# Key and value compression with three products of summed chunks for two neighbouring rows

## The chip, the cores and the metric

One core of one Trainium2 chip runs the whole kernel in one launch. The metric is the device time in microseconds (us), from the median of several runs. Lower is better.

## What is computed

The kernel is one inference step of a decoder with two layers, for a prompt of 512 tokens and for a group of 8 samples with 4 new tokens each, whose past of 2048 tokens lies in pages of 128 tokens. Layer 1 is sparse attention. One of its branches looks at compressed keys and values of the past, and these are computed anew in every step, for each of the 8 samples, from the cached pages:

```python
def compress(x, pos_emb, w1, w2):
    B, L, G, hd = x.shape
    n_chunk = L // CMP_STRIDE
    ch = x[:, :n_chunk * CMP_STRIDE].reshape(B, n_chunk, CMP_STRIDE, G, hd)
    ch = ch.transpose(0, 1, 3, 2, 4).reshape(B, n_chunk, G, CMP_STRIDE * hd)
    half = CMP_STRIDE * hd
    hidden = (ch[:, :-1] @ w1[:half] + ch[:, 1:] @ w1[half:]) + pos_emb.reshape(-1) @ w1
    return jax.nn.gelu(hidden) @ w2
```

Here L is 2048, the stride is 16 tokens, G is 4 heads of 64, so there are 128 chunks with 4 heads each, 1024 numbers long. Row n of the hidden values (256 wide) is chunk n times the first half of w1 plus chunk n+1 times the second half. There are 127 rows for each head. Keys and values each have their own w1 and w2.

## The kernel before

`nsa_compress` (L2043) does this between the prompt's attention and `nsa_decode` (L2225). It works through 16 units: the keys of the 8 samples, then the values of the 8. The order on each engine is written out by hand, and semaphores join them; each engine runs its own list in order.

The reading order `loads` has 18 entries: the key weights, 8 key units, the value weights, 8 value units. Each entry fills one of two slots of the tile `RAWc` (2 MB). A unit's 16 pages come half from SP's queue and half from POOL's (`pages`, L2080); `slot_free` makes a queue wait until the slot's last user has been split. After its own loads, SP also fetches the pages of the selected-block keys of samples 0 and 1 into the tile `KS` (`key_pages`, L2037), which `nsa_decode` reads first.

Each product of 32-bit numbers is made from three products of a high part (a cast to the fp32r type) and a low part (value less high part): high by high, low by high, high by low. ScalarE casts the high part (L2173), VectorE subtracts the low part (L2219). A unit is cut in 8 steps k, each with 128 contraction rows and 512 columns (16 pages x 8 chunks x 4 heads), in tiles `CHi` and `CLo` that hold all 8 steps. The list `jobs` says in which order steps are cut; the value weights' 8 steps alternate with those of the first value unit.

TensorE takes, for each step k, two column halves m of the hidden values and two halves h of w1, three matmuls of 512 or 508 columns (L2150 to L2152), 96 in a unit. They add up in one PSUM bank for each m, and the shift by one chunk between the halves of w1 is an offset of 4 columns. Units alternate between two pairs of banks. After step 5 of unit u TensorE does `project(u - 1)`, the product with w2, which waits for the hidden values of the unit before. A matmul of plain 32-bit operands, as there, shows as two in the trace.

The function between the products, gelu by a tanh formula, goes to and fro: VectorE adds the bias (L2207), ScalarE squares (L2178), VectorE scales and multiplies (L2210, L2211), ScalarE takes the tanh (L2181), VectorE finishes (L2214) and later stores the projected values (L2197, L2199). It is done after step 7 of the next unit has been cut. The tile `self.spent`, shown as CN, holds the middle results. `linear` (L443) is the kernel's common matrix product; its matmuls are L440 and its low parts L434.

## Time and profile before

| | |
|---|---|
| median of 3 runs | 2625.77 us (2624.28 to 2634.29) |
| profiled execution | span 2616.4 us; the page gives no other time for it |
| TensorE matmuls busy | 2229.5 us, 85% of the span |
| VectorE busy | 1201.7 us, 46% |
| ScalarE busy | 584.4 us, 22% |
| GpSimd (POOL) busy | 256.9 us, 10% |

The span goes from the first to the last instruction of the profiled execution. PE is TensorE's matmuls, PEld its weight loads, DVE VectorE, ACT ScalarE, POOL GpSimd, SP the engine whose queue issues most DMAs. In a row of a group of instructions stand the line, the engine, the operation, output and inputs, the shapes and the count, then the busy time in us and the mean of one in ns, then the idle time of the engine ahead of them and what ended it. Shares over the whole span mix many stages, so the rows below are mostly of the stage of `nsa_compress`.

### The profile page before, as it was taken

How to read it: one execution, taken by the hardware profiler on the slowest of the kernel's cores; microseconds unless marked ns; L12 is line 12 of the kernel's file. 1: busy time of each engine (PE TensorE's matmuls, PEld its weight loads, DVE VectorE, ACT ScalarE, POOL GpSimd, SP SyncE). 2: the span in 40 equal slices, each digit the busy share in tenths (PEclk: the TensorE clock that was granted, in tenths of full speed). 3: DMA queues.
4: the chain of work that ended last, by engine and by line, in shares of the span. 5: the costliest groups of instructions: out<-in, count | busy, mean ns of one | idle time of the engine just before them, and what ended most of it. 6: DMA issues, size and time to landing. Idle time of an engine off the chain costs nothing. (4 is left out here: it accounts for less than half of the span.)

```text
span 2616.4 us, 46107 instructions
## 1 busy us (share of the span) xinstructions
PE 2229.5 (85%) x16997; PEld 1935.7 (74%) x16997; DVE 1201.7 (46%) x2137; ACT 584.4 (22%) x1000; POOL 256.9 (10%) x413
## 2 busy tenths in 40 slices
PE   4986737788999897997699969999996776999898
PEld 2863713376999896894598957778873476999898
DVE  4335711155444443436466545565543355444433
ACT  2210300012101001102254545444421212111000
POOL 0100143200000000000022221111202300000000
PEclk8986867898999998997798989999997998999999
DMA  9325099834222321225400033333327812322321
GB/s 359 89 86 211 7 340 386 317 111 156 85 86 86 105 85 33 69 69 226 140 10 1 1 100 95 97 99 96 104 59 291 301 58 65 88 86 85 96 89 57
DMA packets 238959, 321.92 MB, mean 123 GB/s; under 512 B 18235, under 2 KB 196488, under 8 KB 231343
## 3 DMA queue, kind: packets, MB, share of 16 engines
q1 hardware_dynamic: 217495, 241.39, 27.7%
q0 software_dynamic: 21280, 78.14, 8.5%
q8 instruction: 108, 1.77, 0.3%
q14 instruction: 76, 0.62, 0.1%
HBM read 311.56 MB, written 16.42 MB: 125 GB/s over the span
## 5 line engine op out<-in xcount | busy, mean ns | idle before, releaser
L440 PE MATMUL ps<-XHup,WHup 128*128 128x272 f32 x1408 | 292.9, 289 | 17.0 <-DVE XLup L414 13.4
L440 PE MATMUL ps<-XHup,WLup 128*128 128x272 f32 x1408 | 292.3, 289 | 0.0
L440 PE MATMUL ps<-XLup,WHup 128*128 128x272 f32 x1408 | 291.5, 289 | 0.0
L440 PEld LDWEIGHTS ps<-XHup,WHup 128*128 128x128 f32 x1408 | 222.5, 189 | 19.8 <-DVE XLup L414 14.2
L440 PEld LDWEIGHTS ps<-XLup,WHup 128*128 128x128 f32 x1408 | 222.5, 190 | 0.0
L2150 PE MATMUL ps<-CHi,W1H 128*128 128x512 f32 (+1 forms) x512 | 203.3, 397 | 20.7 <-DVE CLo L2219 20.7
L440 PEld LDWEIGHTS ps<-XHup,WLup 128*128 128x128 f32 x1408 | 221.0, 190 | 0.0
L2219 DVE TENSOR_TENSOR CLo<-RAWc,CHi 128x512 fp32r<-128x512 f32 x128 | 140.2, 1116 | 154.2 <-ACT CHi L2173 154.1
L2151 PE MATMUL ps<-CLo,W1H 128*128 128x512 f32 (+1 forms) x512 | 201.7, 394 | 0.0
L2152 PE MATMUL ps<-CHi,W1L 128*128 128x512 f32 (+1 forms) x512 | 200.8, 392 | 0.0
L2173 ACT CAST CHi<-RAWc 128x512 fp32r<-128x512 f32 x128 | 143.6, 1153 | 146.1 <-PE ps L2152 127.4
L440 PE MATMUL ps<-GH,WHdn 128*128 128x272 f32 x704 | 148.3, 292 | 16.6 <-remote 7.4
L433 DVE CAST WHup<-RAWup 128x1024 fp32r<-128x1024 f32 x88 | 61.1, 694 | 218.9 <-DMA RAWup<-in_w_up 163.7
L440 PE MATMUL ps<-GL,WHdn 128*128 128x272 f32 x704 | 147.5, 291 | 0.0
L440 PE MATMUL ps<-GH,WLdn 128*128 128x272 f32 x704 | 146.8, 290 | 0.0
L440 PE MATMUL ps<-XHin,WHin 128*128 128x272 f32 x576 | 123.4, 296 | 22.8 <-issue 13.8
L1442 ACT ACTIVATE P<-ps,NM 128x128 f32<-128x128 f32 (+1 forms) x224 | 100.5, 458 | 168.8 <-DVE NM L1478 166.2
L2150 PEld LDWEIGHTS ps<-CHi,W1H 128*128 128x128 f32 x512 | 96.9, 189 | 48.7 <-DVE CLo L2219 22.7
L1478 DVE TENSOR_REDUCE NM<-ps 128x1 f32<-128x128 f32 (+1 forms) x224 | 89.2, 402 | 84.8 <-PE ps L1382 44.2
L440 PEld LDWEIGHTS ps<-GH,WHdn 128*128 128x128 f32 x704 | 112.4, 192 | 17.5 <-issue 17.5
L440 PE MATMUL ps<-XHin,WLin 128*128 128x272 f32 x576 | 121.8, 294 | 0.0
L440 PE MATMUL ps<-XLin,WHin 128*128 128x272 f32 x576 | 121.6, 293 | 0.0
(488 smaller groups left out, 4116.8 us busy)
## 6 DMA issues: line engine op xcount, KB each, us to landing
RAWup<-in_w_up SPq DMA_DIRECT2D x88, 512.0 KB, 3.9
Wearly<-in_w_mod SPq DMA_DIRECT2D x24, 1024.0 KB, 11.3
RAWdn<-in_w_down SPq DMA_DIRECT2D x14, 1408.0 KB, 6.4
KP<-in_cache_fox_k POOLq DMA_DIRECT2D x64, 256.0 KB, 6.1
KP<-in_cache_fox_k SPq DMA_DIRECT2D x64, 256.0 KB, 12.1
VP<-in_cache_fox_v POOLq DMA_DIRECT2D x64, 256.0 KB, 5.8
VP<-in_cache_fox_v SPq DMA_DIRECT2D x64, 256.0 KB, 12.4
RAWin<-in_nsa_w_in SPq DMA_DIRECT2D x20, 512.0 KB, 3.7
```

The lines of the kernel that those rows point to most:

```text
L433: link(self.nc.vector.tensor_copy(hi, values))
L440: mm = self.nc.tensor.matmul(self.ps[:, banks + n, 0:HALF], w, x[:, n * HALF:(n + 1) * HALF], start=start, stop=stop)
L1442: nc.scalar.activation(P3[:, n % 4, 0:w], ps[:, made[step] % S_BANKS, 0:w], ACT.Exp, bias=NM[:, n:n + 1]).then_inc(sems["bank_read"], 1)
L1478: nc.vector.tensor_reduce(NM[:, n:n + 1], ps[:, made[step] % S_BANKS, 0:width(*units[n])], AX.X, ALU.max, negate=True).then_inc(sems["maxi ...
L2150: nc.tensor.matmul(out, WH[:, kw, w], hi, start=(k == 0 and h == 0), stop=False, skip_group_check=True)
L2151: nc.tensor.matmul(out, WH[:, kw, w], lo, start=False, stop=False, skip_group_check=True)
L2152: last = nc.tensor.matmul(out, WL[:, kw, w], hi, start=False, stop=end, skip_group_check=True)
L2173: nc.scalar.copy(hi, raw).then_inc(high, 1)
L2219: nc.vector.tensor_tensor(lo, raw, hi.bitcast(F32), ALU.subtract).then_inc(cut, 1)
```

## The change

Two neighbouring rows are computed together. Let A be the first half of w1 and B the second, c an even chunk, d the odd chunk after it and c' the next even chunk. The even row is cA + dB and the odd row is dA + c'B. With three products, (c + d)A, d(B - A) and (d + c')B, the even row is the first plus the second, and the odd row is the third less the second. Each product has 256 columns (64 pairs of chunks, 4 heads).

- Weights: three sets A, B and B - A are cut into high and low parts. The difference is made by VectorE.
- Chunks: VectorE's `mix` first makes the two sums for a quarter of a unit (two steps k) in the new tile `S13`, with one addition of 512 elements, two of 192 and one of 120 elements, since a pair's next chunk may be in the next head group or page. Then ScalarE casts the sums and the odd chunks (`high_part`) and VectorE subtracts both (`low_part`). In a page, even and odd chunks lie one float apart, so they are read at steps of 2 floats; before, the pages were read in steps of 8 floats.
- The cut chunks are in a ring of three quarters instead of tiles for a whole unit.
- TensorE does 9 matmuls of 256 columns for each step k and half m instead of 6 of 512 or 508: 144 in a unit. A unit has three PSUM banks, and `project(u - 1)` comes after the third of four quarters and has operands of 128 columns.
- Between: ScalarE takes the product with B - A from PSUM, once with the bias and once with its sign turned (`middle`), VectorE adds the other two (`collect`), then one operation each on 1024 elements: `square`, `scale`, `bend`, `finish`, and ScalarE's `store`. They are spread over quarters 1, 2 and 3 of the next unit.
- The raw slots are now the two halves of `KS`. The selected-block pages can therefore be fetched only when their half has been cut for the last time; SP fetches those of sample 0, POOL those of sample 1.

```diff
-        PAGES, KU = PAST // PAGE, 8
+        PAGES, KU, QU = PAST // PAGE, 8, 4
+        RING, MIX = 3, 2
...
+        jobs = [(x, q) for q in range(QU) for x in range(2)] + [(1 + u, q) for u in range(1, NB) for q in range(QU)]
+        jobs += [(NB + 1 + x, q) for q in range(QU) for x in range(2)] + [(NB + 2 + u, q) for u in range(1, NB) for q in range(QU)]
...
+        RAW = KS[:, :, :, :].rearrange("p s n f -> p s (n f)")
         with self.stage() as (sb, sem):
-            WH, WL = sb("W1H", [P, 2 * KU, 256], F32R), sb("W1L", [P, 2 * KU, 256], F32R)
-            RAW = sb("RAWc", [P, SLOTS, SLOT])
-            CH, CL = (sb(n, [P, KU, 512], F32R) for n in ("CHi", "CLo"))
+            WH, WL = (sb(n, [P, 3, KU, 256], F32R) for n in ("W1H", "W1L"))
+            CH, CL = (sb(n, [P, RING, 2, 768], F32R) for n in ("CHi", "CLo"))
+            S13 = sb("S13", [P, MIX, 2, 512])
+            HID = sb("HIDc", [P, 2, 512])
+            XG, UG = sb("XGc", [P, 2, 512]), self.spent[:, 0:1024].rearrange("p (o m n) -> p o m n", o=2, m=2)
+            VG = self.spent[:, 0:1024].rearrange("p (m n) -> p m n", m=2)
...
             def slot_free(engine, r):
                 if r >= SLOTS:
-                    engine.wait_ge(cut, order[r - SLOTS, KU - 1] + 1)
+                    engine.wait_ge(cut, order[r - SLOTS, QU - 1] + 1)
...
+            def weights_raw(r, q):
+                return RAW[:, r % SLOTS, :].rearrange("p (h k n) -> p h k n", h=2, k=KU)[:, :, 2 * q:2 * q + 2, :]
+            def chunks_raw(r, q):
+                return RAW[:, r % SLOTS, :].rearrange("p (n k c e) -> p k e n c", n=PAGES, k=KU, e=2)[:, 2 * q:2 * q + 2, :, :, :]
+            def difference(n):
+                return S13[:, n % MIX, :, :].rearrange("p k n -> p (k n)")[:, 0:512]
+            def weights_cut(T, q):
+                return T[:, 2, 2 * q:2 * q + 2, :].rearrange("p k n -> p (k n)"), T[:, 0:2, 2 * q:2 * q + 2, :]
+            def chunks_cut(T, d):
+                slot = T[:, d % RING, :, :]
+                return slot[:, :, 0:512], slot[:, :, 512:768].rearrange("p k (n c) -> p k n c", c=16)
...
                         else:
                             pages(sp, r, 0, full)
-                    for b in range(2):
-                        self.key_pages(sp, b, KS[:, b, :, :], ks_full[b])
+                    slot_free(sp, len(loads))
+                    self.key_pages(sp, 0, KS[:, 0, :, :], ks_full[0])
                 @block.gpsimd
                 def _(pool):
...
                         if x[0] == "c":
                             slot_free(pool, r)
                             pages(pool, r, PAGES // 2, pool_full)
+                    slot_free(pool, len(loads) + 1)
+                    self.key_pages(pool, 1, KS[:, 1, :, :], ks_full[1])
                         v = units[j][1]
...
+                        hid = HID[:, :, :].rearrange("p m (g c) -> p m g c", g=4)
+                        pe.wait_ge(ready, j + 1)
+                        if j >= 1:
+                            pe.wait_ge(stored, j)
                         if v == 0:
...
+                            for g in range(4):
+                                rows, columns = slice(g % 2 * HD, g % 2 * HD + HD), slice(g // 2 * P, g // 2 * P + P)
+                                for m in range(2):
+                                    last = nc.tensor.matmul(ps[rows, 6, columns], W2[:, 0, m, :], hid[:, m, g, :],
                                                             start=(m == 0), stop=(m == 1))
                         else:
                             for g in range(4):
                                 for m in range(2):
...
+                                    last = nc.tensor.matmul(ps[:, 7, g * HD:(g + 1) * HD], hid[:, m, g, :], W2[:, 1, m, :],
                                                             start=(m == 0), stop=(m == 1))
                         last.then_inc(projected, 1)
...
+                    for u in range(2 * NB):
                         if u >= 2:
...
+                            pe.wait_ge(summed, u - 1)
+                        for q in range(QU):
+                            d = QU * u + q
+                            pe.wait_ge(cut, order[loads.index(("c", u)), q] + 1)
+                            for kk in range(2):
+                                k = 2 * q + kk
+                                for bank, sig, at in ((0, 0, 0), (2, 1, 256), (1, 2, 512)):
+                                    hi, lo = (T[:, d % RING, kk, at:at + 256] for T in (CH, CL))
+                                    for m in range(2):
+                                        w = slice(m * P, (m + 1) * P)
+                                        out = ps[:, 3 * (u % 2) + bank, m * 256:(m + 1) * 256]
+                                        nc.tensor.matmul(out, WH[:, sig, k, w], hi, start=(k == 0 and m == 0), stop=False, skip_group_check=True)
+                                        nc.tensor.matmul(out, WH[:, sig, k, w], lo, start=False, stop=False, skip_group_check=True)
+                                        last = nc.tensor.matmul(out, WL[:, sig, k, w], hi, start=False, stop=(k == KU - 1), skip_group_check=True)
+                            last.then_inc(used, 1)
+                            if q == 2 and u:
                                 project(u - 1)
                     project(2 * NB - 1)
                 @block.scalar
                 def _(act):
...
+                    def high_part(r, q):
+                        n = order[r, q]
+                        act.wait_ge(mixed, n + 1)
+                        if loads[r][0] == "w":
+                            if loads[r][1]:
+                                act.wait_ge(used, QU * (NB - 1) + q + 1)
+                            a, b = weights_cut(WH, q)
+                            nc.scalar.copy(a, difference(n))
+                            nc.scalar.copy(b, weights_raw(r, q)).then_inc(high, 1)
+                        else:
+                            d = QU * loads[r][1] + q
+                            if d >= RING:
+                                act.wait_ge(used, d - RING + 1)
+                            a, b = chunks_cut(CH, d)
+                            nc.scalar.copy(a, S13[:, n % MIX, :, :])
+                            nc.scalar.copy(b, chunks_raw(r, q)[:, :, 1, :, :]).then_inc(high, 1)
+                    def middle(j):
+                        v = units[j][1]
+                        act.wait_ge(used, QU * (j + 1))
+                        if j:
+                            act.wait_ge(ready, j)
                         for m in range(2):
...
+                            for o in range(2):
+                                last = nc.scalar.activation(UG[:, o, m, :], ps[:, 3 * (j % 2) + 1, m * 256:(m + 1) * 256], ACT.Identity,
+                                                            bias=PB[:, v, m:m + 1], scale=1.0 - 2.0 * o)
+                        last.then_inc(spread, 1)
+                    def square(j):
+                        act.wait_ge(summed, j + 1)
+                        nc.scalar.activation(VG, XG[:, :, :], ACT.Square, scale=0.044715 ** 0.5).then_inc(squared, 1)
+                    def bend(j):
+                        act.wait_ge(scaled, j + 1)
+                        nc.scalar.activation(VG, VG, ACT.Tanh, scale=GELU_C).then_inc(tanh, 1)
+                    def store(j):
+                        b, v = units[j]
+                        act.wait_ge(projected, j + 1)
+                        if v == 0:
+                            nc.scalar.copy(KC[:, b, :, :], ps[:, 6, 0:256].rearrange("p (g c) -> p g c", g=2)[:, :, 0:NCMP]).then_inc(stored, 1)
+                        else:
+                            nc.scalar.copy(VC[:, b, :], ps[0:NCMP, 7, 0:256]).then_inc(stored, 1)
+                    for r, q in jobs:
+                        high_part(r, q)
+                        u = loads[r][1] if loads[r][0] == "c" else 0
+                        if u and q == 1:
+                            if u >= 2:
+                                store(u - 2)
+                            middle(u - 1)
+                        if u and q == 2:
+                            square(u - 1)
+                        if u and q == 3:
+                            bend(u - 1)
+                    store(2 * NB - 2)
+                    middle(2 * NB - 1)
+                    square(2 * NB - 1)
+                    bend(2 * NB - 1)
+                    store(2 * NB - 1)
                 @block.vector
                 def _(dve):
...
+                    def mix(n):
+                        r, q = jobs[n]
+                        if q == 0:
+                            dve.wait_ge(full[r % SLOTS], by_sp[r])
+                            if loads[r][0] == "c":
+                                dve.wait_ge(pool_full[r % SLOTS], by_pool[r])
+                        if n >= MIX:
+                            dve.wait_ge(cut, n - MIX + 1)
+                        if loads[r][0] == "w":
+                            raw = weights_raw(r, q)
+                            nc.vector.tensor_tensor(difference(n).rearrange("p (k n) -> p k n", k=2), raw[:, 1, :, :], raw[:, 0, :, :],
+                                                    ALU.subtract).then_inc(mixed, 1)
                         else:
...
+                            raw, out = chunks_raw(r, q), S13[:, n % MIX, :, :].rearrange("p k (s n c) -> p k s n c", s=2, c=16)
+                            even, odd = raw[:, :, 0, :, :], raw[:, :, 1, :, :]
+                            nc.vector.tensor_tensor(out[:, :, 0, :, :], even, odd, ALU.add)
+                            pairs = [x.rearrange("p k n (g c) -> p k n g c", c=4) for x in (out[:, :, 1, :, :], odd, even)]
+                            for kk in range(2):
+                                to, left, right = (x[:, kk, :, :, :] for x in pairs)
+                                nc.vector.tensor_tensor(to[:, :, :, 0:3], left[:, :, :, 0:3], right[:, :, :, 1:4], ALU.add)
+                            to, left, right = pairs
+                            nc.vector.tensor_tensor(to[:, :, 0:PAGES - 1, :, 3], left[:, :, 0:PAGES - 1, :, 3], right[:, :, 1:PAGES, :, 0],
+                                                    ALU.add).then_inc(mixed, 1)
+                    def low_part(n):
+                        r, q = jobs[n]
                         dve.wait_ge(high, n + 1)
...
+                        if loads[r][0] == "w":
+                            (ah, bh), (al, bl) = weights_cut(WH, q), weights_cut(WL, q)
+                            nc.vector.tensor_tensor(al, difference(n), ah.bitcast(F32), ALU.subtract)
+                            nc.vector.tensor_tensor(bl, weights_raw(r, q), bh.bitcast(F32), ALU.subtract).then_inc(cut, 1)
+                        else:
+                            d = QU * loads[r][1] + q
+                            (ah, bh), (al, bl) = chunks_cut(CH, d), chunks_cut(CL, d)
+                            nc.vector.tensor_tensor(al, S13[:, n % MIX, :, :], ah.bitcast(F32), ALU.subtract)
+                            nc.vector.tensor_tensor(bl, chunks_raw(r, q)[:, :, 1, :, :], bh.bitcast(F32), ALU.subtract).then_inc(cut, 1)
+                    def collect(j):
+                        dve.wait_ge(spread, j + 1)
+                        by_chunk = XG[:, :, :].rearrange("p m (g n c o) -> p o m n g c", g=4, c=4, o=2)
+                        for o in range(2):
+                            for m in range(2):
+                                products, differences = (x.rearrange("p (n g c) -> p n g c", g=4, c=4) for x in (
+                                    ps[:, 3 * (j % 2) + 2 * o, m * 256:(m + 1) * 256], UG[:, o, m, :]))
+                                last = nc.vector.tensor_tensor(by_chunk[:, o, m, :, :, :], products, differences, ALU.add)
+                        last.then_inc(summed, 1)
+                    def scale(j):
+                        dve.wait_ge(squared, j + 1)
+                        nc.vector.scalar_tensor_tensor(VG, VG, 1.0, XG[:, :, :], ALU.add, ALU.mult).then_inc(scaled, 1)
+                    def finish(j):
+                        dve.wait_ge(tanh, j + 1)
+                        if j:
+                            dve.wait_ge(projected, j)
+                        nc.vector.scalar_tensor_tensor(HID[:, :, :], VG, 1.0, XG[:, :, :], ALU.add, ALU.mult).then_inc(ready, 1)
+                    nc.vector.memset(S13[:, :, :, :], 0.0).then_inc(zeroed, 1)
+                    dve.wait_ge(zeroed, 1)
+                    mix(0)
+                    for n, (r, q) in enumerate(jobs):
+                        if n + 1 < len(jobs):
+                            mix(n + 1)
+                        low_part(n)
+                        u = loads[r][1] if loads[r][0] == "c" else 0
+                        if u and q == 1:
+                            collect(u - 1)
+                        if u and q == 2:
+                            scale(u - 1)
+                        if u and q == 3:
+                            finish(u - 1)
+                    collect(2 * NB - 1)
+                    scale(2 * NB - 1)
+                    finish(2 * NB - 1)
```

Lines taken away that the functions above show are mostly left out of it.

## Rows read from the trace of the kernel before

**Rows 1.** Busy time by engine in one key unit (PE, PEld, DVE, ACT, POOL, clock, DMA).

```profile
1705.86:1729.96 24.10, 24.10 (x106) 18.45 (x104) 13.89 (x19) 11.49 (x12) 0.00 (x0) 1.00 0.27 88
```

**Rows 2.** Timeline of VectorE, bias adds: start, length, engine, operation.

```profile
1705.86 1.42 DVE L2207 TENSOR_SCALAR XGc<-ps,PB 128x512 f32<-128x512 f32 x2
...
1729.96 1.42 DVE L2207 TENSOR_SCALAR XGc<-ps,PB 128x512 f32<-128x512 f32 x2
...
1907.72 1.41 DVE L2207 TENSOR_SCALAR XGc<-ps,PB 128x512 f32<-128x512 f32 x2
...
1933.31 1.38 DVE L2207 TENSOR_SCALAR XGc<-ps,PB 128x512 f32<-128x512 f32 x2
```

**Rows 3.** Waits in the stage: who for whom, us, times, longest.

```profile
ACT CHi L2173 <- PE ps L2152: 127.4, 64, 6.9
```

**Rows 4.** Timeline of TensorE around a key unit's projection.

```profile
1647.39 1.99 PE L2129 MATMUL ps<-XGc,W 128*64 128x254 f32 x8
1649.31 0.50 PE L2150 MATMUL ps<-CHi,W1H 128*128 128x512 f32 x1
```

**Rows 5.** Busy time of line L440 alone (PE, PEld), in layer 1's last part.

```profile
2350.00:2360.00 10.00, 10.00 (x82) 10.00 (x82) 1.00 0.22 64
```

**Rows 6.** Groups of VectorE by shape, whole span: busy us, mean ns, idle.

```profile
L2219 DVE TENSOR_TENSOR CLo<-RAWc,CHi 128x512 fp32r<-128x512 f32 x128 | 140.2, 1116 | 154.2 <-ACT CHi L2173 154.1
L434 DVE TENSOR_TENSOR WLup<-RAWup,WHup 128x1024 fp32r<-128x1024 f32 x88 | 107.8, 1225 | 12.1
...
L1498 DVE TENSOR_TENSOR T<-ps,RC 128x256 f32<-128x256 f32 x32 | 13.6, 425 | 4.4
...
L2219 DVE TENSOR_TENSOR W1L<-RAWc,W1H 128x512 fp32r<-128x512 f32 x16 | 10.5, 693 | 16.4 <-ACT W1H L2173 16.4
```

**Rows 7.** Timeline of VectorE: queued operations, and one behind a result.

```profile
1553.05 4.90 DVE L2219 TENSOR_TENSOR W1L<-RAWc,W1H 128x512 fp32r<-128x512 f32 x8 [16.38 <-ACT W1H L2173]
...
1957.03 0.42 DVE L2210 TENSOR_SCALAR CN<-CN 128x512 f32<-128x512 f32 x1
1957.58 0.69 DVE L2211 TENSOR_TENSOR CN<-CN,XGc 128x512 f32<-128x512 f32 x1
```

**Rows 8.** Groups of ScalarE by shape, whole span.

```profile
L2173 ACT CAST CHi<-RAWc 128x512 fp32r<-128x512 f32 x128 | 143.6, 1153 | 146.1 <-PE ps L2152 127.4 <-DMA RAWc<-in_cache_nsa_vc 13.4 <-DMA RAWc<-in_cache_nsa_kc 5.2
...
L1442 ACT ACTIVATE P<-ps,NM 128x256 f32<-128x256 f32 x40 | 19.0, 474 | 14.6 <-DVE NM L1478 13.8
...
L2173 ACT CAST W1H<-RAWc 128x512 fp32r<-128x512 f32 x16 | 9.2, 614 | 13.5 <-DMA RAWc<-in_nsa_cmp_w_k 13.5
...
L1885 ACT COPY VE<-TOK 128x1024 f32<-128x1024 f32 x2 | 2.0, 1044 | 0.8 <-PEq L116 0.8
```

**Rows 9.** Timelines of VectorE, POOL and ScalarE at the switch to values.

```profile
1728.60 1.13 DVE L2219 TENSOR_TENSOR CLo<-RAWc,CHi 128x512 fp32r<-128x512 f32 x1 [1.62 <-ACT CHi L2173]
...
1730.94 0.54 POOL L2080 DMA_DIRECT2D RAWc<-in_cache_nsa_vc  x1 [39.35 <-issue]
1732.08 0.54 POOL L2080 DMA_DIRECT2D RAWc<-in_cache_nsa_vc  x1 [0.61 <-issue]
...
1741.69 1.17 ACT L2173 CAST CHi<-RAWc 128x512 fp32r<-128x512 f32 x1 [6.67 <-DMA RAWc<-in_cache_nsa_vc]
```

**Rows 10.** Timelines of POOL, ScalarE and TensorE at the stage's start.

```profile
1551.05 0.54 POOL L2080 DMA_DIRECT2D RAWc<-in_cache_nsa_kc  x1 [0.60 <-issue]
...
1552.40 4.26 ACT L2173 CAST W1H<-RAWc 128x512 fp32r<-128x512 f32 x8 [13.53 <-DMA RAWc<-in_nsa_cmp_w_k]
...
1558.98 0.80 PE L2150 MATMUL ps<-CHi,W1H 128*128 128x512 f32 x1 [20.74 <-DVE CLo L2219]
```

**Rows 11.** Busy time by engine at the start; the clock follows POOL's count.

```profile
1559.00:1580.00 21.00, 21.00 (x85) 17.17 (x86) 13.80 (x13) 12.78 (x12) 8.58 (x16) 0.92 0.70 201
```

**Rows 12.** Timeline of VectorE: the stage's last store, and decoding's first key scores.

```profile
1964.91 0.42 DVE L2199 COPY VC<-ps 127x256 f32<-127x256 f32 x1 [4.08 <-PE ps L2134]
...
1991.25 1.22 DVE L2509 TENSOR_REDUCE BM<-ps 128x16 f32<-128x1024 f32 x1 [2.61 <-PE ps L2337]
```

96 lines of the change are left out of this document (2 added, 94 removed).

## The prediction

> **What bounds the kernel now.** The changed method, `nsa_compress`, runs from about 1552 to 1967 us of the span. I read first the busy times of one of its units (one slot's keys or values of one sample; there are 16). In the 24.1 us of a key unit TensorE is busy all the time, at a granted clock of 1.00, while VectorE is busy 13.9, ScalarE 11.5 [rows 1]. The start of the bias add, once in each unit, gives the period: 24.1 us for a key unit, 25.6 us for a value unit [rows 2]. Inside the stage ScalarE's longest wait in total is for TensorE to give chunk tiles back, 127.4 us in 64 waits [rows 3]: the two elementwise engines are ahead, and TensorE sets the pace. A key unit's projection costs TensorE 1.9 us (from its first matmul to the next of the main ones [rows 4]), so the 96 main matmuls take 22.2, 0.231 us each at 510 columns. A value unit's projection is 1.5 us longer by its period, about 3.5 us.
>
> **TensorE's part.** Three products of 256 columns replace two passes of about 510 over two banks: for each of 8 k and 2 halves 9 matmuls of 256 columns instead of 6, so 144 in a unit instead of 96. The nearest rows are `linear`'s matmuls, 272 columns with the same 128x128 weights and type: 82 in 10 us, 0.122 each, with weight loads that hide [rows 5]. Between that and 0.231 at 510 columns a column costs 0.46 ns, so 256 columns cost 0.115 us. If the weight load became the limit it could be no dearer than at 272, 0.122: bounds 0.115 to 0.122. I take 0.115: 16.6 us in a unit, 4.15 in a quarter (the new step, 36 matmuls). With the projection TensorE needs 18.6 us for a key unit and 20.1 for a value unit, where it had 24.1 and 25.6.
>
> **VectorE's part.** A contiguous subtraction of 512 elements takes 693 ns and one of 1024 takes 1225, so about 1.04 ns an element over 0.16 [rows 6]. The old chunk subtraction, with the same 512 elements, takes 1116: its input goes in steps of 8 floats (32 bytes). The new inputs step by 2 floats. No row shows this step. The bounds are 693 and 1116; I take the contiguous price for the long runs, since two steps still lie beside each other, and a third of the surcharge for the pieces of three. Queued one behind the other, operations start 0.08 us earlier than their durations say (8 in 4.90 us); behind a wait on a result they start about 0.13 later [rows 7].
> `mix` of a chunk quarter: 0.69 for 512 elements, two of 192 at 0.40, one of 120 in steps of 16 and 32 bytes at 0.38, less overlap 0.25, plus a wait 0.1: 1.7 us. `low_part`: 1.23 + 0.69, less 0.08, plus 0.1: 1.9. A quarter is 3.6, four are 14.5. `collect`: four of 256 from PSUM at 0.425 [rows 6], 1.5; `scale` and `finish` 1.3 each. In all 18.6 us a unit, against 13.9 before. On the disputed step the Trainium skill says (SBUF — State Buffer, on SBUF cachelines) that accesses keep full rate while at least two fall in one 16-byte line; by it a step of 8 bytes is free and one of 32 is not, which agrees with the 1116 ns, and the sum stays as made; without it, at the 32-byte price, it would be that of the third rival.
>
> **ScalarE's part.** A quarter is one copy of 1024 (1.04) and one of 512, 0.61 contiguous or 1.15 with wide steps [rows 8]: 1.65. `middle` is four of 256 from PSUM, at 0.47 by the nearest row less overlap 1.6; square and tanh 1.1 each, `store` 0.4. Together 10.8 to 13 us a unit, hidden.
>
> **The path through all three.** There are now buffers for only three quarters instead of a whole unit, and TensorE's projection of unit u-1 stands between quarters 2 and 3 of unit u, behind `finish`, which VectorE does only after the low part of quarter 3. So a ring closes: `finish` 1.3, projection 2.0, quarter 3 on TensorE 4.15, `middle` 1.6, `collect` 1.5, `mix` 1.7, `low_part` 1.9, `scale` 1.3, `mix` 1.7, `low_part` 1.9, and three hand-overs between engines 0.45: 19.5 for keys, 21.0 for values. It is a little above both engines' own sums. With 0.3 to 0.5 for waits that don't fit: 19.8 and 21.5.
>
> **The switch to values.** Slot 0 for the first value pages is given back by the last low part of unit 7. Before, the last subtraction ended at 1729.73, POOL issued eight pages 1.15 us apart, and the first chunk cast began at 1741.69 [rows 9]: 12.0 us. TensorE didn't feel it, with up to a unit cut ahead. Now it has at most two quarters (8 us) and, where VectorE sets the pace, one. So unit 8 is 12.0 for the load, then 6.3 for the first pair of quarters (chunks 3.6, weights 0.7 + 1.9, rounded), three pairs 18.8, `collect` and `scale` 2.8: 39.9 us.
>
> **Start.** Weights land at 1552.4, the first matmul is at 1559.0. Now `mix` of the chunk quarter waits for the first pages as well, whose last issue is at 1551.1 [rows 10]; some 4 us to landing, my estimate from the 12.0 us above less eight issues, make it 1555; then 1.7, the weights' low part 1.9, a `mix` 0.6, the chunks' low part 1.9: 1561.1. The zeroing of S13 lies under the load. TensorE's slow first stretch (granted clock 0.92 over 21 us, so 1.7 us lost [rows 11]) is now covered by the pairs that it waits for. Unit 0 is three pairs, 18.8.
>
> **End.** From the last low part: `finish` 1.3, projection of unit 14 3.5, quarter 3 4.15, then a bare tail: `middle` 1.6, `collect` 1.5, square 1.1, `scale` 1.3, tanh 1.1, `finish` 1.3, the last projection 3.5 and 0.4 until its last result is out, `store` 0.4, hand-overs 0.6: 12.8. POOL's 16 key pages start at that last low part and take 16 times 1.15, 18.4 us; the rest takes 21.8, so POOL ends 3 us before it. SP's wait for its slot is over one unit earlier, and only its 16 page issues stand behind it. In the decode method POOL's window and value gathers and SP's window keys queue behind these issues, which are done. The last pages land about when decoding starts, and before the change VectorE read the first scores of these keys at 1991.3, 26 us after the stage's end [rows 12]. If that cover were gone it would cost the 3 us of a landing. I allow 1 us for DMA collisions there.
>
> **Sum.** 1561.1 + 18.8 + 7 x 19.8 + 39.9 + 7 x 21.5 + 1.3 + 3.5 + 4.15 + 12.8 = 1930.7, against 1965.3 now [rows 12]: 34.6 us sooner, 33.6 with the collisions. The span of 2616.4 becomes 2582.8. The profile gives the execution's span only; the median of the runs, 2625.77, stands 9.4 above it, and I carry that over: 2592 us, 1.3% faster.
>
> **Rivals.**
> 1. TensorE keeps the pace (the pieces of VectorE's work overlap better than in my ring). Then units cost 18.6 and 20.1: 7 x 1.2 + 7 x 1.4 = 18 less, and the buffered quarter takes 4 off the switch: 2570. For it: the two sums are within 1 us of each other. Against it: a ring with three buffers has nothing to average over.
> 2. Matmuls of 256 columns cost 0.122: 144 x 0.007 = 1.0 a unit, 14 of them and the quarters at the end, but partly under the ring: up to 2606. Then still faster. For it only that the load is as long as the matmul's pitch.
> 3. The other side: steps of 8 bytes cost as much as steps of 32. The 512 pieces rise by 0.42 each (one in `mix`, one in `low_part`), the short ones by 0.25 together: 1.1 a quarter, 4.4 a unit on VectorE, 23.0 in all. TensorE then waits in each unit. Units 23.3 and 23.9, 7 x 3.5 + 7 x 2.4 = 41, and 7 for units 0 and 8: 48 us more, 2640, 0.5% slower than before. It decides as soon as a 512 addition takes above 1.0 us. For it: the old cast and subtraction paid 1.6 to 1.9 times the price; against it: four times less distance. If each of two such inputs paid separately (1.5 us for the 512 addition), 2680.
> 4. The change doesn't do what it says: TensorE's work doesn't fall, since 256 columns cost more than 0.15 us. The 0.122 at 272 columns [rows 5] speaks against it.
>
> **How the numbers follow.** My forecast 0.50 (2578 to 2606); rival 1 0.18; rival 2 0.06; rival 3 0.20, of this a quarter beyond 2650 and two fifths within 0.5% of before (a partial price); rival 4 0.06. A difference below 0.5%, 13 us, can hardly be told from none here. Below 2612.6 lie the forecast, rivals 1 and 2: 0.76 with a little of rival 3; within 0.5% 0.12; slower 0.12. Leaving out 0.2, the range goes from 2562 (rival 1 less another 8 for the switch, should it be hidden in full) to 2625. The forecast's own range is 2578 to 2606.
>
> **What would show it.** In the profile after: main matmuls starting 0.115 us apart; VectorE the busiest engine of the stage by share or level with TensorE, near 0.9; additions of 512 at about 0.69; periods of 19.8 and 21.5 us; a gap of about 12 us on TensorE at unit 8; the stage's end near 1931; TensorE's idle time put down to the chunk low part and to `HIDc`. I am wrong if the additions take over 1 us, if projections wait longer than a ring of 21 us allows, or if POOL's last page issue ends the stage.

## The result, and the profile after

The changed kernel takes 2586.67 us (median of 4 runs, 2581.14 to 2587.71), the kernel before 2627.24 (4 runs, 2624.28 to 2634.29): a ratio of 0.9853, 95% interval 0.9821 to 0.9885, so 1.5% faster. The prediction was 2592.

The profiled execution of the kernel after, its page:

```profile
span 2585.8 us, 48102 instructions
...
PE 2156.4 (83%) x17829; PEld 1929.8 (75%) x17829; DVE 1260.5 (49%) x2354; ACT 572.2 (22%) x1048; POOL 264.4 (10%) x429
...
L2160 PE MATMUL ps<-CHi,W1H 128*128 128x256 f32 x768 | 223.7, 291 | 50.2 <-DVE CLo L2268 50.2
```

This execution's own time is 2587.51 us: 1.7 lie around the span. I compare the stage from the start of the last matmuls of L1392 ahead of it to the `MEMSET QB` with which decoding begins: 1537.62 to 1967.41 before, 429.8 us, and 1545.09 to 1935.20 after, 390.1 us. That is 39.7 less, as much as the medians' 40.6. The spans differ by 30.6 only, because the unchanged code ahead of the stage took 7.5 us longer in this execution and decoding to the end 1.6 longer.

One key unit and one value unit of the kernel after, busy time by engine (PE, PEld, DVE, ACT, POOL, clock, DMA), against [rows 1]:

```profile
1628.16:1646.70 18.54, 18.54 (x163) 18.23 (x161) 16.75 (x30) 10.37 (x16) 4.28 (x9) 1.00 0.38 114
1827.25:1846.31 19.06, 19.06 (x163) 19.06 (x162) 16.73 (x31) 10.36 (x16) 4.24 (x8) 1.00 0.38 108
```

TensorE is busy all the time, as before, and VectorE's 16.7 us fit under it. The periods are 18.54 us for keys and 19.06 for values, where [rows 2] give 24.1 and 25.6.

The kernel after, timeline of VectorE: `mix` at the first pages, at unit 1, two `collect`s, `mix` at the first and second value pages, decoding's first operation, its first key scores:

```profile
1564.64 0.69 DVE L2248 TENSOR_TENSOR S<-KS 128x512 f32<-128x512 f32 x1 [3.62 <-DMA KS<-in_cache_nsa_kc]
...
1597.55 0.69 DVE L2248 TENSOR_TENSOR S<-KS 128x512 f32<-128x512 f32 x1 [12.13 <-DMA KS<-in_cache_nsa_kc]
...
1609.62 1.42 DVE L2277 TENSOR_TENSOR XGc<-ps,CN 128x256 f32<-128x256 f32 x4 [2.09 <-ACT CN L2194]
...
1628.16 1.42 DVE L2277 TENSOR_TENSOR XGc<-ps,CN 128x256 f32<-128x256 f32 x4 [1.78 <-ACT CN L2194]
...
1740.74 0.69 DVE L2248 TENSOR_TENSOR S<-KS 128x512 f32<-128x512 f32 x1 [10.58 <-DMA KS<-in_cache_nsa_vc]
...
1775.52 0.69 DVE L2248 TENSOR_TENSOR S<-KS 128x512 f32<-128x512 f32 x1 [11.81 <-DMA KS<-in_cache_nsa_vc]
...
1935.20 0.91 DVE L2542 MEMSET QB<- 128x1024 f32 x1 [6.54 <-PEq L116]
...
1959.31 1.23 DVE L2592 TENSOR_REDUCE BM<-ps 128x16 f32<-128x1024 f32 x1 [3.75 <-PE ps L2420]
```

The waits of 10.58 and 12.13, 11.81 us are of one kind: VectorE stands with the next chunks' pages not landed. Only the first was foreseen, at the switch; the other two are for the pages of units 1 and 9.

The kernel after, timeline of TensorE: the first matmul, the first one of unit 0's last quarter, three steady starts, the first one of unit 8, the projection of unit 7 (before unit 8's last quarter), and the last projection:

```profile
1570.44 0.58 PE L2160 MATMUL ps<-CHi,W1H 128*128 128x256 f32 x1 [24.40 <-DVE CLo L2268]
...
1600.88 0.58 PE L2160 MATMUL ps<-CHi,W1H 128*128 128x256 f32 x1 [14.22 <-DVE CLo L2268]
...
1649.82 0.28 PE L2162 MATMUL ps<-CHi,W1L 128*128 128x256 f32 x1
1649.94 0.28 PE L2160 MATMUL ps<-CHi,W1H 128*128 128x256 f32 x1
1650.06 0.28 PE L2161 MATMUL ps<-CLo,W1H 128*128 128x256 f32 x1
...
1746.63 0.55 PE L2160 MATMUL ps<-CHi,W1H 128*128 128x256 f32 x1 [8.88 <-DVE CLo L2268]
...
1779.98 2.03 PE L2138 MATMUL ps<-HIDc,W 128*64 128x128 f32 x16 [14.53 <-DVE HIDc L2288]
...
1928.71 3.67 PE L2143 MATMUL ps<-W,HIDc 128*128 128x64 f32 x16 [7.81 <-DVE HIDc L2288]
```

Main matmuls start 0.120 us apart. Each of VectorE's page waits comes through to TensorE, 14.22, 8.88 and 14.53 us. For 14.22 and 14.53 the way there is VectorE's list, in which `mix` of the next quarter stands ahead of `low_part` of this one: at 1597.55 VectorE still owes the low part of unit 0's last quarter, whose matmuls start at 1600.88, and at 1775.52 that of unit 8's last quarter and `finish` of unit 7, for which the projection waits. So in these two TensorE stands although the chunks that it needs have long landed. No run tries the other order.

Behind each of these waits, and at the start, TensorE first works at a granted clock of 0.50, the lower of its two levels (1.2 GHz), in which main matmuls start 0.213 us apart. Busy time by engine of the kernel after, from 1600.88:

```profile
1600.88:1606.67 5.79, 5.79 (x27) 5.79 (x28) 5.76 (x11) 1.63 (x2) 2.14 (x4) 0.50 0.50 152
```

In all TensorE works 22.3 us of the stage at this level before its last projection. By the two pitches that work would take some 9.7 us less at 1.00; this is an estimate, and how much of it the stage gets longer by was not taken apart. The last projection, 3.67 us, is at 0.50 too, behind a wait of 7.81 us; one in the steady units takes half of that.

Groups by shape in the stage of the kernel after (busy us, mean ns), to be held against [rows 6, 8]:

```profile
L2267 DVE TENSOR_TENSOR CLo<-S,CHi 128x1024 fp32r<-128x1024 f32 x64 | 77.8, 1216 | 0.0
...
L2252 DVE TENSOR_TENSOR S<-KS 128x192 f32<-128x192 f32 x128 | 44.4, 388 | 0.0
L2248 DVE TENSOR_TENSOR S<-KS 128x512 f32<-128x512 f32 x64 | 44.0, 688 | 38.8 <-DMA KS<-in_cache_nsa_vc 22.4 <-DMA KS<-in_cache_nsa_kc 15.7
L2268 DVE TENSOR_TENSOR CLo<-KS,CHi 128x512 fp32r<-128x512 f32 x64 | 43.7, 684 | 0.0
...
L2143 PEld LDWEIGHTS ps<-W,HIDc 128*128 128x128 f32 x128 | 16.6, 209 | 8.0 <-DVE HIDc L2288 8.0
```

The additions and subtractions of 512 elements with 8-byte steps take 688 and 684 ns, the price of contiguous ones (693 in [rows 6]), not the 1116 of the 32-byte step. The Trainium skill ("SBUF — State Buffer", on SBUF cachelines) has two accesses in one 16-byte line at full rate: the trace agrees. And the value projection's weight load, 209 ns here, took 327 in the kernel before, which matters below. (The 209 is a mean over two clocks: 192 in seven projections, 330 in the last.)

### The profile page after: what moved, and what is told of

The parts are those of the page before. It is cut to its first block and busy times, and to the rows that moved or that the text cites. A ratio compares the mean times of both kernels' runs of the same rounds, so it can differ in the third digit from the quotient of the medians.

```text
span 2585.8 us, 48102 instructions
## 1 busy us (share of the span) xinstructions
PE 2156.4 (83%) x17829; PEld 1929.8 (75%) x17829; DVE 1260.5 (49%) x2354; ACT 572.2 (22%) x1048; POOL 264.4 (10%) x429
## 3 DMA queue, kind: packets, MB, share of 16 engines
q8 instruction: 115, 1.88, 0.3%
## 5 line engine op out<-in xcount | busy, mean ns | idle before, releaser
L440 PE MATMUL ps<-XHup,WHup 128*128 128x272 f32 x1408 | 293.5, 290 | 17.3 <-DVE XLup L414 13.8
L440 PE MATMUL ps<-XHup,WLup 128*128 128x272 f32 x1408 | 293.1, 290 | 0.0
L440 PE MATMUL ps<-XLup,WHup 128*128 128x272 f32 x1408 | 292.1, 289 | 0.0
L2160 PE MATMUL ps<-CHi,W1H 128*128 128x256 f32 x768 | 223.7, 291 | 50.2 <-DVE CLo L2268 50.2
L440 PEld LDWEIGHTS ps<-XHup,WHup 128*128 128x128 f32 x1408 | 223.3, 190 | 20.2 <-DVE XLup L414 14.6
L440 PEld LDWEIGHTS ps<-XLup,WHup 128*128 128x128 f32 x1408 | 223.0, 190 | 0.0
L440 PEld LDWEIGHTS ps<-XHup,WLup 128*128 128x128 f32 x1408 | 221.6, 190 | 0.0
L2161 PE MATMUL ps<-CLo,W1H 128*128 128x256 f32 x768 | 221.3, 288 | 0.0
L2162 PE MATMUL ps<-CHi,W1L 128*128 128x256 f32 x768 | 221.1, 288 | 0.0
L2160 PEld LDWEIGHTS ps<-CHi,W1H 128*128 128x128 f32 x768 | 151.6, 197 | 53.0 <-DVE CLo L2268 42.4
L440 PE MATMUL ps<-GH,WHdn 128*128 128x272 f32 x704 | 148.2, 292 | 16.6 <-remote 14.7
L2161 PEld LDWEIGHTS ps<-CLo,W1H 128*128 128x128 f32 x768 | 151.7, 198 | 0.0
L2162 PEld LDWEIGHTS ps<-CHi,W1L 128*128 128x128 f32 x768 | 151.4, 197 | 0.0
L440 PE MATMUL ps<-GL,WHdn 128*128 128x272 f32 x704 | 147.1, 291 | 0.0
L440 PE MATMUL ps<-GH,WLdn 128*128 128x272 f32 x704 | 146.5, 290 | 0.0
L440 PE MATMUL ps<-XHin,WHin 128*128 128x272 f32 x576 | 123.1, 296 | 21.2 <-issue 12.0
L440 PEld LDWEIGHTS ps<-GH,WHdn 128*128 128x128 f32 x704 | 112.2, 191 | 17.5 <-issue 17.5
L440 PE MATMUL ps<-XHin,WLin 128*128 128x272 f32 x576 | 121.9, 294 | 0.0
L440 PE MATMUL ps<-XLin,WHin 128*128 128x272 f32 x576 | 121.6, 293 | 0.0
```

Source lines behind the costliest of these rows:

```text
L440: mm = self.nc.tensor.matmul(self.ps[:, banks + n, 0:HALF], w, x[:, n * HALF:(n + 1) * HALF], start=start, stop=stop)
L2160: nc.tensor.matmul(out, WH[:, sig, k, w], hi, start=(k == 0 and m == 0), stop=False, skip_group_check=True)
L2161: nc.tensor.matmul(out, WH[:, sig, k, w], lo, start=False, stop=False, skip_group_check=True)
L2162: last = nc.tensor.matmul(out, WL[:, sig, k, w], hi, start=False, stop=(k == KU - 1), skip_group_check=True)
```

## The experiments

Executions of one kernel differ by more than some of these effects (the kernel before, 15 executions alongside the last two kernels below: 2610.78 to 2639.77). For kernels that ran once I therefore read periods and the stage's length, not the total.

**Weights first.** Both slots are taken in unit 0: one by the weights, one by the first chunks. `jobs` takes them by turns, so the weights' slot comes free only with the last quarter, and unit 1's pages start then. With the value weights and unit 8 it is the same, and unit 9's pages start late. This kernel cuts all weights ahead of the chunks, both times:

```diff
-jobs = [(x, q) for q in range(QU) for x in range(2)] + ...
-jobs += [(NB + 1 + x, q) for q in range(QU) for x in range(2)] + ...
+jobs = [(x, q) for x in range(2) for q in range(QU)] + ...
+jobs += [(NB + 1 + x, q) for x in range(2) for q in range(QU)] + ...
```

> The four weight quarters are cut before the first chunk quarter, for keys and for values, instead of in turn with it. Theory A (three waits for pages, 12.1 us at unit 1, 10.6 at unit 8 and 11.8 at unit 9, come from a slot that the alternating order gives back late, and TensorE has too few cut quarters to bridge them): the waits at units 1 and 9 go, the one at unit 8 stays near 10 us but the value weights are cut inside it; the first matmul comes about 3.4 us later; the step from unit 0 to unit 1 falls by about 10, at the switch by 2 and at unit 9 by 12. Time about 24 us below the changed kernel, near 2563 us. Theory B (the page waits are hidden, and the two units with weights are long because VectorE has 6.2 us of work for each pair of quarters): the same work in another order, so the time stays within 5 us of the changed kernel, near 2587 us.

Measured: 2553.3 us (2549.55 to 2560.08), ratio to the kernel before 0.9726, interval 0.9676 to 0.9775. Its waits on pages in the stage (total us, times, longest):

```profile
DVE S L2248 <- DMA KS<-in_cache_nsa_vc: 4.1, 2, 3.4
DVE S L2248 <- DMA KS<-in_cache_nsa_kc: 2.9, 1, 2.9
```

and TensorE's wait for low parts (its first matmul's included):

```profile
PE ps L2160 <- DVE CLo L2268: 39.5, 2, 29.6
```

The stage is 358.2 us, 31.9 less than in the changed kernel; 24 were expected. `collect` of unit 0 comes 51.4 us after the stage's beginning, where it was 64.5, though the first matmul is 5.3 us later; at the switch VectorE's page waits fall from 22.4 to 4.1. The periods stay 18.54. So the waits for the pages of units 1 and 9 are the cost of the order of the jobs. The one at the switch leaves VectorE, which now cuts the value weights meanwhile, but not TensorE, which still stands 9.9 us ahead of unit 8. Of the 31.9 us, 25.0 are idle time of TensorE, and it works 13.4 us less at the granted clock of 0.50, some 6 by the same estimate; the expectation had left the clock out. This kernel beats both.

**The second order alone**, the keys' left as it was:

> The same new order for the value weights alone; the keys keep the alternating order. Theory A: the wait at unit 1 stays at 12 us, the one at unit 9 goes; about 14 us below the changed kernel, near 2573 us. Theory B: no difference above 5 us.

Measured: 2569.88 us (2566.07 to 2570.8), ratio 0.9786 (0.974 to 0.9832), stage 369.4. The values' waits are 4.0 us, the keys' 16.1, the longest 12.1, is still there. The values' order takes 20.7 us off the stage (1.8 of it ahead of `collect` of unit 0, where this kernel is unchanged) and the keys' the other 11.2. The places show it: the switch (`collect` of unit 6 to that of unit 8) takes 68.3 us in the changed kernel, 49.3 here and 49.5 with both orders, and `collect` of unit 0 comes at 64.5, 62.8 and 51.4. The keys' order alone was not run.

**Less for VectorE: no short sums.** Leaves out the two additions of 192 elements in each quarter (part of the neighbour sums isn't computed):

```diff
-for kk in range(2):
-    to, left, right = (x[:, kk, :, :, :] for x in pairs)
-    nc.vector.tensor_tensor(to[:, :, :, 0:3], left[:, :, :, 0:3], right[:, :, :, 1:4], ALU.add)
```

> The two additions of 192 elements in each chunk quarter are left out, so three quarters of the second sums are zeros and the compressed rows are not the right ones; all else is as in the changed kernel. VectorE saves about 0.6 us a quarter, 2.4 a unit. Theory A (TensorE sets the period): periods of key and value units stay at 18.5 and 19.1 us, and VectorE's wait for ScalarE's middle results grows from 1.8 us by about 2.4. Theory B (the ring of engines sets it, as the prediction had it): two mix steps lie in the ring, so the periods fall by about 1.2 us, the span by about 17.

Measured: 2573.88 us once. A key unit, busy time by engine:

```profile
1619.46:1637.99 18.53, 18.53 (x162) 18.23 (x161) 14.42 (x22) 10.29 (x16) 4.29 (x8) 1.00 0.40 114
```

and VectorE's wait for `middle` in the stage:

```profile
DVE XGc L2274 <- ACT CN L2194: 64.8, 15, 11.0
```

VectorE is busy 2.3 us less in a unit and the period doesn't move; it waits 64.8 us for `middle` where it waited 39.4. The stage is 7.1 us shorter, all of it outside the steady units (4.8 before `collect` of unit 0, 2.4 at the switch). In the steady units VectorE and the path through all three engines aren't the limit.

**More for VectorE.** The 512 addition of `mix` is done twice, the second behind a wait on the first, 0.82 us a quarter:

```diff
+nc.vector.tensor_tensor(out[:, :, 0, :, :], even, odd, ALU.add).then_inc(twice, 1)
+dve.wait_ge(twice, chunks_seen[0] + 1)
+chunks_seen[0] += 1
```

> The addition of 512 elements is made twice in each chunk quarter, the second behind a wait on the first: 0.69 + 0.13 = 0.82 us more a quarter, 3.3 a unit. Theory A (TensorE sets the period at 18.5 us, VectorE has 1.8 us to spare in it): VectorE becomes the bound, 16.8 + 3.3 = 20.1 us for a key unit, 20.1 to 20.3 for a value unit, the span about 20 us longer. Theory B (the ring sets it): two of the four additions lie in the ring, so 1.6 us more than now in each, 20.2 and 20.7, about 24 us. So this run tells how near the other bound is, and less which theory holds.

Measured: 2601.25 us once, periods 19.61 and 19.67, stage 408.1. A key unit, busy time by engine:

```profile
1648.75:1668.37 19.62, 18.63 (x162) 18.25 (x162) 19.45 (x36) 10.36 (x16) 4.29 (x8) 1.00 0.37 104
```

Keys and values now take nearly the same time, and VectorE is busy 19.45 of the 19.62 us: the limit has gone over to it. The second addition made VectorE's busy time only 2.7 us longer, not 3.3, and the period 1.07: the 1.8 us that VectorE had waited for `middle` were free. Both theories had put the period at 20 us or more.

**A ring of two quarters** (`RING = 2`):

> Two quarter buffers instead of three. Theory A (TensorE sets the period and three buffers are just enough): ScalarE's cast now waits for the quarter that TensorE ended one earlier, and the casts behind middle come too late once a unit; key periods of 19.5 to 21 us, the span 20 to 35 us longer. Theory B (buffers don't matter, only the sums of the engines do): periods stay at 18.5 and 19.1 us.

Measured: 2596.47 us once, periods 19.40 and 20.13, stage 403.9. ScalarE's wait for TensorE to give a quarter back:

```profile
ACT CHi L2184 <- PE ps L2162: 136.3, 54, 9.1
```

With two buffers the engines do close a ring: in a key unit TensorE stands 0.8 us ahead of the projection and VectorE waits 2.6 us for a cast that TensorE holds up. It costs 0.9 to 1.1 us a unit, a little less than theory A had.

**Fewer columns for the low parts.** The two products with low parts take 192 of the 256 columns (so some sums lack their low parts):

```diff
-nc.tensor.matmul(out, WH[:, sig, k, w], lo, ...)
-last = nc.tensor.matmul(out, WL[:, sig, k, w], hi, ...)
+nc.tensor.matmul(out[:, 0:192], WH[:, sig, k, w], lo[:, 0:192], ...)
+last = nc.tensor.matmul(out[:, 0:192], WL[:, sig, k, w], hi[:, 0:192], ...)
```

> The two matmuls with a low part, of every three, take 192 columns instead of 256, so for 64 columns of each product the low parts are left out. Matmuls of 256 columns start 0.120 us apart in the changed kernel, where the prediction had 0.115. Theory A (the columns set the pitch, near 0.46 ns each): the shorter ones start 0.09 us apart; TensorE's work falls by 96 x 0.03 = 2.9 us a unit and the period falls to what VectorE or the ring allows, about 17.5. Theory B (the weight load sets the pitch at 256 columns): all stay near 0.120 and the period stays at 18.5 us.

Measured: 2572.94 us once, stage 377.5, periods 17.63 and 18.16. Timeline of TensorE:

```profile
1650.20 0.30 PE L2160 MATMUL ps<-CHi,W1H 128*128 128x256 f32 x1
1650.34 0.25 PE L2161 MATMUL ps<-CLo,W1H 128*128 128x192 f32 x1
1650.43 0.28 PE L2162 MATMUL ps<-CHi,W1L 128*128 128x192 f32 x1
1650.55 0.30 PE L2160 MATMUL ps<-CHi,W1H 128*128 128x256 f32 x1
```

The starts are 0.114 us apart in the mean, neither 0.120 nor the 0.098 that columns alone would give (213 in the mean, 0.46 ns each). In four key units they are 0.142 behind a matmul of 256 columns and 0.091 and 0.110 behind those of 192. TensorE stays busy for all of the 17.63 us, and 144 times 0.0063 is the 0.91 by which the period fell. So TensorE sets it, and its pitch follows columns only in part.

**Where the short projection comes from.** In the changed kernel a value unit is only 0.52 us longer than a key unit. Two kernels ask why, and a third further down. First 127 columns of hidden values as weights instead of 128, in the changed kernel:

```diff
-nc.tensor.matmul(ps[:, 7, ...], hid[:, m, g, :], W2[:, 1, m, :], ...)
+nc.tensor.matmul(ps[0:NCMP, 7, ...], hid[:, m, g, 0:NCMP], W2[:, 1, m, :], ...)
```

> The value projection takes 127 columns of hidden values as its weights, as before the change, but at unit stride from the new tile, where the changed kernel takes 128. In the changed kernel one of its weight loads takes 209 ns, before the change it took 327 at 127 columns with a step of 4 floats. Theory A (the count of 127 is what made it slow): loads of about 320 ns, a projection of about 3.5 us instead of 1.8, a value unit of 20.8 us instead of 19.1, the span 12 to 14 us longer. Theory B (the step made it slow): loads near 209 ns and no change.

Then the other way round, 128 columns in the kernel before, where they lie 4 floats apart in `XGc`:

```diff
-matmul(ps[0:NCMP, 5, ...], hid[:, m, g // 2, g % 2, 0:NCMP], W2[:, 1, m, :], ...)
+matmul(ps[:, 5, ...], hid[:, m, g // 2, g % 2, 0:128], W2[:, 1, m, :], ...)
```

> The kernel before with one edit: the value projection takes 128 columns of hidden values instead of 127, at the old step of 4 floats. If the count of 127 made its weight loads slow (327 ns), they fall to about 210, the projection from 3.5 to about 1.8 us, and the kernel gets 12 to 14 us faster, 0.5%: a third of what the whole change brought would then be this. If the step made them slow, nothing changes.

The value projection's weight loads by shape, in the changed kernel with 127:

```profile
L2143 PEld LDWEIGHTS ps<-W,HIDc 128*127 128x127 f32 x128 | 16.5, 209 | 8.0 <-DVE HIDc L2288 8.0
```

and in the kernel before with 128:

```profile
L2134 PEld LDWEIGHTS ps<-W,XGc 128*128 128x128 f32 x128 | 30.5, 327 | 5.3 <-DVE XGc L2214 5.0
```

Measured: 2580.97 us once, value period 19.05; and 2623.29 us (2616.47 to 2635.57), ratio 0.9998 (0.9971 to 1.0024). The count changes nothing in either kernel. What differs is the layout. By clock the loads are, in the changed kernel in seven steady projections (granted clock 1.00) and in the last (0.50), and in the last of the kernel before (0.50):

```profile
L2143 PEld LDWEIGHTS ps<-W,HIDc 128*128 128x128 f32 x112 | 13.1, 192 | 0.0
...
L2143 PEld LDWEIGHTS ps<-W,HIDc 128*128 128x128 f32 x16 | 3.5, 330 | 8.0 <-DVE HIDc L2288 8.0
...
L2134 PEld LDWEIGHTS ps<-W,XGc 128*127 128x127 f32 x16 | 3.8, 328 | 5.0 <-DVE XGc L2214 5.0
```

The contiguous load follows the clock; the stepped one takes 327 ns at 1.00 and 328 at 0.50.

**Parts of the change put into the kernel before.** First its raw buffers alone: `RAW` lies in the halves of `KS`, and the key pages wait for their slots.

```diff
-RAW = sb("RAWc", [P, SLOTS, SLOT])
+RAW = KS[:, :, :, :].rearrange("p s n f -> p s (n f)")
...
+slot_free(sp, len(loads))
+self.key_pages(sp, 0, KS[:, 0, :, :], ks_full[0])
...
+slot_free(pool, len(loads) + 1)
+self.key_pages(pool, 1, KS[:, 1, :, :], ks_full[1])
```

> The kernel before with one part of the change alone: the two raw slots are the halves of KS, and the selected-block pages are fetched when their half is free, sample 0 by SP, sample 1 by POOL. Theory A (this part moves no time: the chunk tiles hold a whole unit, so the last raw slot is cut some 20 us before the stage ends, and POOL's 18.4 us of issues fit): stage length within 2 us of 429.8, ratio within noise of 1. Theory B (POOL's issues delay decoding): 3 to 10 us slower.

Measured: 2624.65 us (2606.88 to 2631.51), ratio 0.9997 (0.9969 to 1.0025). The moved key pages cost nothing that shows. The profiled stage is 438.1 us, where 429.8 within 2 was expected; what makes it longer is told below. Then, on top of it, the hidden values in a tile of their own, head by head, so that the projections read them without a step:

```diff
+HID = sb("HIDc", [P, 2, 512])
-hid = XG[:, :, :].rearrange("p m (c gp e) -> p m gp e c", gp=2, e=2)
+hid = HID[:, :, :].rearrange("p m (gp e c) -> p m gp e c", gp=2, e=2)
-scalar_tensor_tensor(XG[:, m, :], UG[:, m, :], 1.0, XG[:, m, :], ...)
+scalar_tensor_tensor(HID[:, m, :].rearrange("p (g c) -> p c g", g=4), a, 1.0, b, ...)
```

> The kernel before with the pages in KS and one more edit: VectorE's last gelu operation writes the hidden values head by head to a tile of their own, so the projection reads them at unit stride; 127 columns as before. Theory A (the step of 4 floats made the projection's weight loads slow, 327 ns, and unit stride brings them to 209): the projection of a value unit falls from 3.5 to about 1.8 us, value periods from 25.6 to 23.9, key periods from 24.1 to between 23.3 and 24.1; the span 12 to 18 us shorter, a third or more of what the whole change brought. VectorE's operation gets dearer by its wide output step, up to 1.15 us, hidden. Theory B (something else in the new layout, such as the bank or the unit's order, made them fast): periods stay.

Measured: 2601.16 us (2595.5 to 2605.19), ratio 0.9919 (0.9893 to 0.9944): 0.8 of the change's 1.5%, without one product less. Timeline of TensorE with the hidden values 4 floats apart (key pages in `KS`), around a value unit's projection:

```profile
1848.15 3.71 PE L2136 MATMUL ps<-W,XGc 128*127 128x64 f32 x16
...
1852.72 0.63 PE L2152 MATMUL ps<-CHi,W1H 128*128 128x508 f32 x1
1853.15 0.63 PE L2153 MATMUL ps<-CLo,W1H 128*128 128x508 f32 x1
...
1856.32 0.39 PE L2153 MATMUL ps<-CLo,W1H 128*128 128x512 f32 x1
1856.55 0.40 PE L2154 MATMUL ps<-CHi,W1L 128*128 128x512 f32 x1
```

The same kernel, busy time by engine just behind that projection:

```profile
1852.42:1854.42 2.00, 2.00 (x6) 1.54 (x5) 0.00 (x0) 0.00 (x0) 0.00 (x0) 0.50 0.00 0
```

And the timeline of TensorE with the plain layout:

```profile
1836.68 1.88 PE L2137 MATMUL ps<-W,HIDc 128*127 128x64 f32 x16
```

The layout does two things. The projection itself takes 1.88 us instead of 3.71 for values and 1.08 instead of 1.99 for keys. Keys read the hidden values as the moving operand, not as weights; their matmuls, kernel before and plain layout:

```profile
L2129 PE MATMUL ps<-XGc,W 128*64 128x254 f32 x64 | 15.9, 631 | 0.0
...
L2132 PE MATMUL ps<-HIDc,W 128*64 128x254 f32 x64 | 8.6, 390 | 0.0
```

And with the step the granted clock falls to 0.50, 1.2 GHz, right behind a value projection of 3.71 us: for about 3.4 us matmuls of 508 columns start 0.43 us apart instead of 0.23, which makes the unit 27.2 us instead of 25.6. It doesn't happen at each projection: in one of six value periods of the kernel before as profiled, in four of six with 128 columns, in five of six with `RAW` in `KS`. With hidden values read without a step, in the nine kernels profiled, no steady value unit was granted less than 1.00. What decides when it happens stays open. With the plain layout value units take 23.8 us at most. The stage is 438.1 us in the first of the two kernels and 408.5 in the second. VectorE pays 1113 ns for the scattered write, under TensorE.

Against this last kernel the changed one shows what the three products and the order that comes with them do in the stage: its twelve steady periods are 55.4 us shorter together, `collect` of unit 0 comes 17.1 us later, the switch takes 20.9 us longer and the end 1.0 less, 18.4 us in all. More than half of what the products save is lost at the two places where weights are cut.

## Why the prediction was right

The total was right, 2586.67 against 2592 and within the forecast's own range of 2578 to 2606, but in part by luck: the steady units came out 22.2 us shorter than forecast, the beginning and the switch 19.3 us longer, and the two nearly cancelled. In the steady units the mechanism was the first rival's, not the forecast's. The marks in the table are the starts of `collect`. The predicted ones come from the prediction's own terms, with 10.0 us from the start of `collect` to the unit's last low part (1.5 + 1.7 + 1.9 + 1.3 + 1.7 + 1.9) and 2.1 from the last store to decoding, as before:

| Stretch | predicted us | measured us | difference |
|---|---|---|---|
| stage's beginning to `collect` of unit 0 | 52.1 | 64.5 | +12.4 |
| six key periods | 118.8 | 111.2 | -7.6 |
| `collect` of unit 6 to that of unit 8 (switch) | 61.4 | 68.3 | +6.9 |
| six value periods | 129.0 | 114.4 | -14.6 |
| `collect` of unit 14 to decoding | 33.9 | 31.7 | -2.2 |
| sum | 395.2 | 390.1 | -5.1 |

- **"A ring closes ... units 19.8 and 21.5"** failed. TensorE keeps the pace, as rival 1 had it: 18.54 and 19.06. Taking work from VectorE changes no period, two quarters instead of three raise it to 19.4, and shorter matmuls lower it to 17.63. So the ring of three, with a TensorE quarter 0.2 us shorter, lies below 17.6 us, where I had 19.5. One round of it in the kernel after, from `collect` at 1628.16 to `collect` at 1646.70:

```profile
1637.14 1.22 DVE L2288 SCALAR_TENSOR_TENSOR HIDc<-CN,XGc 128x1024 f32<-128x1024 f32 x1
...
1639.41 1.15 PE L2138 MATMUL ps<-HIDc,W 128*64 128x128 f32 x16
1640.48 0.39 PE L2160 MATMUL ps<-CHi,W1H 128*128 128x256 f32 x1
...
1645.10 1.57 ACT L2194 ACTIVATE CN<-ps,PB 128x256 f32<-128x256 f32 x4 [3.29 <-PE ps L2162]
```

  VectorE takes 8.98 us from `collect` to `finish`, where the terms have 10.0; the projection takes 1.07, where they have 2.0; quarter 3 with its hand-over takes 4.62 and `middle` 1.60, about as predicted. And between the end of `finish` (1638.36) and the projection lie 1.05 us in which TensorE is still at quarter 2: the ring is open by about as much, and some 17.5 us long.
- **The projection, "2.0 for keys, 3.5 for values"**, was carried over from a kernel with stepped hidden values. Measured by the period less 144 times 0.120: 1.26 and 1.78. The prediction didn't cost what the `HIDc` layout does to its reader, though the diff shows it. Put alone into the kernel before, the layout gives half as much as the change gains on the whole. Only the last projection takes the 3.5 us forecast, 3.67, and for another reason, a granted clock of 0.50.
- **The pitch, 0.115 with bounds 0.115 to 0.122**: 0.120, near rival 2's bound, 0.7 us a unit. This and the short projection cancel in a key unit, so that TensorE's 18.6 looks right there; for values 20.1 was 1.0 too much.
- **Unit 0 "is three pairs, 18.8", unit 9 an ordinary 21.5**: failed. The pages behind the weights, too, are loaded in the open when weights and chunks are cut in turns: 12.13 us at unit 1, 11.81 at unit 9. I had followed the slot of unit 8's pages at the switch and not asked what frees the slot that holds weights. The run with weights first takes 31.9 us off the stage, these two waits above all. The granted clock of 0.50 behind each of these waits had no term either.
- **The switch, 12.0 us of load**: right. The first value `mix` starts 11.7 us after unit 7's last low part, and VectorE waits 10.58 of it.
- **The start**: the first matmul at +25.4 us from the stage's beginning, against 23.5 predicted. The first pages are used 5.8 us after POOL's last issue of them (1558.86), not 4. What the 4 was worked out from, 12.0 us less eight issues of 1.15, gives 2.8.
- **VectorE's durations**: right. 688 and 684 for the 512 pieces, 388 for 192, 1216 for 1024, 418 for `collect`; a unit's busy time is 16.75, where 18.6 had 0.8 us of waits in it that don't occur and too little overlap from one operation to the next. Rival 3 (8-byte steps as dear as 32-byte ones) is out, and so is rival 4.
- **The end**: right. POOL issued its last key page at 1929.45, 3 us before the last store, as predicted, and the first key scores come 24.1 us after decoding's start. The kernel before with this part alone runs at a ratio of 0.9997.

POOL's first and last key pages of the kernel after, in its timeline:

```profile
1912.23 0.54 POOL L2041 DMA_DIRECT2D KS<-in_cache_nsa_ks  x1 [27.75 <-issue]
...
1929.45 0.54 POOL L2041 DMA_DIRECT2D KS<-in_cache_nsa_ks  x1 [0.61 <-issue]
```

- **The carry-over of 9.4 us from span to median**: wrong. What lies around the span is 1.7 us, so the execution profiled before took about 2618.1 and was a quick one, 7.7 below the median. The prediction of the span, 2582.8, was 3.0 off. Of the difference of the medians, 33.6 predicted against 40.6, about 7 is missing; the stage accounts for 5.1, and 1.0 had been set aside for collisions.

## What to carry to other kernels

When a change touches the layout of an operand, cost its reader as well as its writer: reading the projection's operand without a step gives here, put in alone, half of what the whole change gains. When two streams share a ring of load slots, follow for each slot what frees it and what is loaded then; consuming both in turns holds both to the end, consuming one first lets its next load run under the other. A wait of TensorE's costs more than its length when a lower clock follows, here 0.213 us a matmul instead of 0.120. And when a sum of terms comes out right, look at the stretches before believing the terms.

## What the runs showed of the hardware

- A weight load of 32-bit hidden values costs 327 ns with 16 bytes from one column to the next and 192 ns when they are contiguous, for 127 columns as for 128, at a granted clock of 1.00. At 0.50 the two cost 328 and 330 ns: the step costs nothing more there. The Trainium skill ("TensorE: Matmul & The Clock Gate", LDWEIGHTS) lets the time of a load depend on its columns alone; the measurement differs. The Trainium skill's demand of two accesses in one 16-byte line ("SBUF — State Buffer", on SBUF cachelines) would explain it, as a step of 16 bytes gives one; no run shows that this is the cause.
- As a moving operand of 254 columns the same values cost 631 ns a matmul with the step and 390 without.
- Behind a stretch of such loads TensorE's granted clock falls to 0.50 for about 3.4 us, in some executions of the unit and not in others. This costs 1.6 us each time. It can be part of what makes executions of the kernel before differ: its profiled stage, 429.8 us, has one such fall in six value periods, and that with `RAW` in `KS`, 438.1 us, has five.
- Pairs of a 128x128 weight load and a matmul in this type start 0.114 us apart with 213 columns in the mean, 0.120 with 256, 0.122 with 272 [rows 5], and 0.231 with 510: below 272 columns the pitch falls far less than in proportion to the columns.
